# Order of the evictions of v and z at the seam between two head pairs of a differential-attention kernel

## The reference

```
proj = u @ w_in                         # 512x2048 @ 2048x8192
q, k = 16 heads of 128 each;  v = 8 heads of 256;  z = 512x2048
logits = q k^T * 128**-0.5 + rel_bias, causal mask
p = softmax(logits)                     # for both heads of a pair
a = p[head 0] - lam * p[head 1]
o = rms_norm(a @ v, subln_g) * (1 - lam_init)
y = (o * silu(z)) @ w_out
out = layer_norm(alpha * u + y, g, b)
```

## Time and profile before

| | before |
|---|---|
| median of 3 runs | 932.64 us (932.06 to 932.73) |
| the profiled execution's own time | 931.81 us |
| its span | 929.6 us |
| TensorE busy (matmul) | 915.0 us, 98% |
| VectorE busy | 609.9 us, 66% |
| ScalarE busy | 381.3 us, 41% |
| GpSimd busy | 177.8 us, 19% |
| chain that ended last | TensorE 93%, VectorE 5%, ScalarE 1% |

### The profile page before, as it was taken

How to read it: one execution, slowest core, us unless ns; L and a number is a source line. 1 busy time by engine, 2 the same in 40 slices (tenths; PEclk the granted TensorE clock), 3 DMA queues, 4 the chain that set the end, 5 groups by cost and what they waited for, 6 DMA issues and landing times.

```text
span 929.6 us, 14281 instructions
## 1 busy us (share of the span) xinstructions
PE 915.0 (98%) x5210; PEld 807.9 (87%) x5210; DVE 609.9 (66%) x1020; ACT 381.3 (41%) x653; POOL 177.8 (19%) x364
## 2 busy tenths in 40 slices
PE   9999999999999999999999999999999899999996
PEld 8888989898989898989898989898989688888885
DVE  5675767676767576757766675768576877435455
ACT  4443445443535354535453444354534544113211
POOL 1200313031303221222122122312131000000032
PEclk9999999999999999999999999999999999999999
DMA  8732506250625062506250625152517324443332
GB/s 305 285 100 88 188 25 203 86 184 33 198 81 186 23 203 77 183 27 199 82 178 31 195 86 174 37 188 73 159 55 258 139 91 135 182 153 111 133 133 93
DMA packets 43274, 124.53 MB, mean 134 GB/s; under 512 B 8160, under 2 KB 10208, under 8 KB 42992
## 3 DMA queue, kind: packets, MB, share of 16 engines
q1 hardware_dynamic: 29328, 97.27, 31.6%
q0 software_dynamic: 9504, 17.75, 6.0%
q10 hardware_dynamic: 4416, 9.18, 2.7%
HBM read 108.01 MB, written 13.15 MB: 130 GB/s over the span
## 4 chain that ended last, share of the span: by engine, by line
PE 93%; DVE 5%; ACT 1%; DMA 0%; issue 0%; SPq 0%; ACTq 0%; DVEq 0%
PE proj L1401 73%; PE att L1401 20%; DVE scratch L1094 1%; DVE w_split L918 1%; ACT w_split L623 1%; DVE scratch L1087 1%; DVE scratch L1079 1%; DMA w_raw<-w_in_tiles_dram 0%; DVE w_split L924 0%; DVE scratch L1041 0%; DVE operands L1227 0%; DVE operands L1035 0%; DVE big L1393 0%; DVE mix L1073 0%; ACT w_split L632 0%
## 5 line engine op out<-in xcount | busy, mean ns | idle before, releaser
L1401 PE MATMUL proj<-w_split,xg_split 128*128 128x512 f32 (+1 forms) x1512 | 294.4, 354 | 0.0
L1401 PEld LDWEIGHTS proj<-w_split,xg_split 128*128 128x128 f32 x1512 | 250.7, 189 | 39.5
L1401 PE MATMUL proj<-xg_split,w_split 128*128 128x512 f32 (+1 forms) x1032 | 204.2, 355 | 2.7 <-DVE scratch L1041 2.1
L1401 PEld LDWEIGHTS proj<-xg_split,w_split 128*128 128x128 f32 x1032 | 171.4, 189 | 32.1 <-issue 4.6
L918 DVE TENSOR_TENSOR w_split<-w_raw,w_split 128x1024 fp32r<-128x1024 f32 x98 | 119.9, 1223 | 96.0 <-ACT w_split L623 94.4
L623 ACT ACTIVATE w_split<-w_raw 128x1024 fp32r<-128x1024 f32 x98 | 103.7, 1058 | 135.5 <-PE proj L1401 128.5
L549 POOL DMA_DIRECT2D scratch<-scratch x224 | 110.3, 501 | 107.5 <-DVE scratch L1094 57.3
L1401 PE MATMUL att<-w_split,xg_split 128*128 128x512 f32 x432 | 99.9, 389 | 0.0
L1401 PEld LDWEIGHTS att<-w_split,xg_split 128*128 128x128 f32 x432 | 81.0, 188 | 16.8
L623 ACT ACTIVATE w_split<-x_res 128x1024 fp32r<-128x1024 f32 x42 | 44.6, 1061 | 106.0 <-PE proj L1401 67.3
L1401 PE MATMUL proj<-w_split,x_sums 128*128 128x256 f32 x672 | 82.9, 283 | 0.0
(11 more groups left out here) (153 smaller groups left out, 825.3 us busy)
## 6 DMA issues: line engine op xcount, KB each, us to landing
w_raw<-w_in_tiles_dram SPq DMA_DIRECT2D x112, 512.0 KB, 3.6
w_raw<-w_out_tiles_dram SPq DMA_DIRECT2D x32, 512.0 KB, 3.3
x_res<-w_in_tiles_dram SPq DMA_DIRECT2D x14, 512.0 KB, 4.2
bias_by_distance<-bias_lines POOLq DMA_DIRECT2D x8, 640.0 KB, 5.0
scratch<-scratch POOLq DMA_DIRECT2D x112, 40.0 KB, 2.6
bias<-bias_by_distance POOLq DMA_DIRECT2D x8, 512.0 KB, 4.0
x_res<-in_x_dram ACTq DMA_DIRECT2D x4, 1024.0 KB, 6.1
big<-x_cols_dram SPq DMA_DIRECT2D x7, 512.0 KB, 9.6
```

Source lines behind the costliest of these rows:

```text
L1401: return nc.tensor.matmul(dst, lhsT, rhs, start=start, stop=stop, skip_group_check=True)
```

## The change

Four edits, and one instruction.

1. In pairs 0 to 6 VectorE evicts the tile of bank 0 first, then does `combine(p, 3)` and `turn_a(p)`, then the tiles of banks 2, 1 and 3 (`VZ_ORDER`). TensorE's waits count in that order. ScalarE's order stays 0, 1, 2, 3.
2. In pair 7 VectorE evicts tiles 0 and 1 before slot 21, and tiles 2 and 3 behind its block's low part; then come the second early piece of g, the low parts of a for two row tiles, `combine(7, 3)` and the transposition of the last row tile.
3. In pair 7 ScalarE evicts the four banks directly behind slot 21, ahead of the high parts of a and of g's second early piece.
4. The first early piece of g goes to slot 20 on both engines: on ScalarE ahead of the exponentials of the last row tile, on VectorE ahead of the first 16 transpositions.
5. GpSimd gets one `drain()` behind its loop over the pairs.

`weigh_v` and `gate` now wait for all four tiles of v and z, since the counter no longer names a tile.

```
+            nc.gpsimd.drain()                       # GpSimd, behind the loop over the pairs
             for s in range(ST):
...
+                if j == 20 and last_pair(p):        # ScalarE, slot
+                    g_early_hi(0)
                 if 17 <= j < 21:
                     exps(p, j - 17)
...
             for j in range(SLOTS):                  # ScalarE, pair 7
                 slot(PAIRS - 1, j)
+            vz_tiles(PAIRS - 1)
             aT_split(PAIRS - 1, 0)
             aT_split(PAIRS - 1, 1)
-            g_early_hi()
-            vz_tiles(PAIRS - 1)
+            g_early_hi(1)
...
             def vz_tiles(p):                        # VectorE
-                for s in range(ST):
-                    ...
+                vz_tile(p, VZ_ORDER[0])
+                combine(p, 3)
+                turn_a(p)
+                for s in VZ_ORDER[1:]:
+                    vz_tile(p, s)
...
-                if j == 21:                         # VectorE, slot
-                    combine(p, 3)
-                    if not last_pair(p):
-                        turn_a(p)
                 if j == 20 and last_pair(p):
+                    g_early_lo(0)
                     turn_last_a(False)
...
-            for j in range(SLOTS):                  # VectorE, pair 7
+            for j in range(SLOTS - 1):
                 slot(PAIRS - 1, j)
+            vz_tile(PAIRS - 1, 0)
+            vz_tile(PAIRS - 1, 1)
+            slot(PAIRS - 1, SLOTS - 1)
+            vz_tile(PAIRS - 1, 2)
+            vz_tile(PAIRS - 1, 3)
+            g_early_lo(1)
             aT_split(PAIRS - 1, 0)
             aT_split(PAIRS - 1, 1)
-            g_early_lo()
-            vz_tiles(PAIRS - 1)
+            combine(PAIRS - 1, 3)
             turn_last_a(True)
...
-                        pe.wait_ge(vz_moved, p * ST - ST + bank + 1)      # TensorE, opening
+                        pe.wait_ge(vz_moved, p * ST - ST + VZ_ORDER.index(bank) + 1)
...
-                pe.wait_ge(vz_moved, p * ST + tiles[-1] + 1)              # TensorE, weigh_v
+                pe.wait_ge(vz_moved, p * ST + ST)
...
+VZ_ORDER = [0, 2, 1, 3]
```

More of the change, by code:

```diff
@@ L797, in slot, with g_early_hi @@
                     q_chunk(p)
+                if j == 20 and last_pair(p):
+                    g_early_hi(0)
                 if 17 <= j < 21:
                     exps(p, j - 17)
-            def g_early_hi():
+            def g_early_hi(i):
                 act.wait_ge(scores_done, PAIRS * ST)
                 act.wait_ge(g_loaded, 16 * (PAIRS - 1))
-                for i in range(EARLY // 2):
-                    nc.scalar.activation(g_early[:, 0, 2 * i:2 * i + 2], g[:, 2 * i:2 * i + 2],
-                                         ACT.Copy).then_inc(g_hi, 1)
+                nc.scalar.activation(g_early[:, 0, 2 * i:2 * i + 2], g[:, 2 * i:2 * i + 2],
+                                     ACT.Copy).then_inc(g_hi, 1)
             def first_split(i):
@@ L1030, in k_chunk, with vz_tile @@
                                             ALU.subtract).then_inc(k_moved, 1)
+            def vz_tile(p, s):
+                dve.wait_ge(vz_hi, p * ST + s + 1)
+                nc.vector.tensor_tensor(v[:, 1, s], vz_banks(p)[:, s, 0:PW], v[:, 0, s].bitcast(F32), ALU.subtract)
+                twice_silu(p, s).then_inc(first_v_moved if first_pair(p) else vz_moved, 1)
             def vz_tiles(p):
-                for s in range(ST):
[L1034 to L1037, removed]
+                vz_tile(p, VZ_ORDER[0])
[3 more added lines that the diff above has]
+                    vz_tile(p, s)
             def twice_silu(p, t):
@@ L1130, in gate @@
                 dve.wait_ge(first_v_moved, ST)
-                dve.wait_ge(vz_moved, n)
+                dve.wait_ge(vz_moved, p * ST + ST)
                 nc.vector.scalar_tensor_tensor(gated_of(p, t), gated_of(p, t), o_scale[:, t:t + 1], silu_z[:, t],
@@ L1182, in first_slot @@
                     w_sum(1, 0, 3)
-                if j == 15:
-                    combine(0, 3)
-                    turn_a(0)
             def slot(p, j):
@@ L1216, in slot, with g_early_lo @@
                     q_chunk(p)
-                if j == 21:
-                    combine(p, 3)
-                    if not last_pair(p):
-                        turn_a(p)
                 if j == 20 and last_pair(p):
+                    g_early_lo(0)
                     turn_last_a(False)
[L1224 to L1229, removed]
+            def g_early_lo(i):
+                dve.wait_ge(g_hi, i + 1)
+                nc.vector.tensor_tensor(g_early[:, 1, 2 * i:2 * i + 2], g[:, 2 * i:2 * i + 2],
+                                        g_early[:, 0, 2 * i:2 * i + 2].bitcast(F32),
+                                        ALU.subtract).then_inc(g_split, 1)
             def first_split(i):
```

## The result

| | before | changed |
|---|---|---|
| median | 932.43 us (932.06 to 932.73, 4 runs) | 920.61 us (920.48 to 920.67, 4 runs) |
| ratio | | 0.9872 (95%: 0.986 to 0.9884) |
| profiled execution, span | 931.81, 929.6 us | 920.48, 918.4 us |
| TensorE busy | 98% | 99% |
| mean granted clock | 0.998 | 1.000 |

The kernel is 1.3% faster, 11.8 us. The direction and the two large terms came out; a third one, the drain, was put at nothing and is worth 2.3 us. The span became 11.2 us shorter, over the 9.5 that the prediction gave as a sign of being wrong.

What follows compares the result with a forecast made beforehand. TensorE, busy 98% of the span, was taken as the bound, losing time at openings that wait for evictions. Gains of 3.72 + 5.42 = 9.14 us off 932.64 gave 923.5 us, range 921.8 to 927.2.

Steps and rivals of the forecast that it cites:

- the two large terms: Gains at TensorE's openings: 3.72 us in the loop (pairs 2 to 7), 5.42 us at the output projection.
- the drain: GpSimd behind the loop: could gain 0 to 3 us, taken as 0; over 0.5 us had a chance of 0.04.
- sign of being wrong: Wrong if the span's gain exceeds 9.5 us or TensorE's idle time returns under another name for more than 2.
- Edit 1: Openings of pairs 2 to 7: TensorE's wait for bank 0 goes, 6 x 0.62 = 3.72 us gained.
- Edits 2 to 4: Output projection's opening: the 3.55 us wait and the half clock behind it go, 5.42 us gained.
- The tie at step (0, 2): Output stage: VectorE's part of g seen at 748.29, TensorE wants it at 748.32; taken as nothing.
- Slot 20's wait for the reads of g: ScalarE in pair 7 waits for all seven reads of g; margin 0.7 us, cost nothing.
- The subtraction from the median: The 9.14 us gain taken off the median, 932.64 us, which is 0.83 above the profiled execution: 923.5.
- Rival A: TensorE's loop jump was hidden by the wait, so the six openings gain nothing: 927.2 us; chance 0.13.
- B: The last opening's wait moves to step (0, 2): 924.5 to 927.4 us; chance 0.12.
- C: Slower: reads of g land late for ScalarE in slot 20, 933 to 935 us at 10.5 late; chance 0.02.
- D: Loop openings wait for bank 2's tile instead, at worst six times 0.2 us left: 924.7 us; chance 0.05.

Runs made afterwards that it cites:

- e5: Edit 1 alone on the kernel before, without the drain: 928.63 us against 932.41, ratio 0.9959.
- e6: Edits 2 to 4 alone on the kernel before, the loop's evictions as before, no drain: 926.47 us against 932.41.
- e8: The changed kernel with VectorE's first late part of g ahead of its second 16 transpositions: 920.33 us against 920.50.
- e1: The kernel before with the drain alone: 930.38 us against 931.89 on the same chip, ratio 0.998.
- e2: The changed kernel without its drain: 922.86 us.
- e4: The changed kernel with its drain behind pair 3 of GpSimd's loop instead of behind pair 7: 926.23 us.
- e3: The changed kernel with its drain moved to GpSimd's beginning, ahead of every DMA that GpSimd issues: 923.04 us.

## Why the prediction was wrong, point by point

- **Edit 1**, 3.72 us: right. e5 is 3.8 us faster by its medians; in the chain each opening is continuous, and bank 2's tile ended 0.5 us before it was wanted, 0.4 with the semaphore's 0.12 taken off as the forecast did (0.35).
- **Edits 2 to 4**, 5.42 us: right in mechanism and, in the profiled execution, in size. The idle 3.55 is gone and so is the half clock (e6). What I took for a fixed 1.87 us varies from execution to execution; 7.31 and 8.46 us were seen for the same 24 matmuls. "Otherwise it is 1.00" stands in no row shown, but the trace bears it out: the clock is 1.00 but for 741.1 to 744.5 us and the last 0.8 us of the span, behind the work.
- **The tie at step (0, 2)**: "which I take as nothing" was 0.22 us, shown by e8. The second transpositions started 5.6 us behind the output stage's first matmul (738.25 against 732.66; forecast 741.87 against 736.41).
- **Slot 20's wait for the reads of g**: nothing, as said; ScalarE's L807 starts at 723.01, straight behind its block.
- **The drain** is the step that failed. The prediction put it: "Could it gain? [...] 0 to 3 us. I take 0, since GpSimd's rows show it waiting for others only." It is worth 2.3 us (e1, e2), a case that had a chance of 0.04, and with 0 in its place the range's lower end was 921.8. Without its drain the changed kernel takes 922.86 us (e2), inside the range. The reason given was no reason: GpSimd's rows say what it did up to its last instruction, and the question was what followed it. The rows to read were there: GpSimd's last end at 923.90, the last DMA activity at 926.2, the span's end at 929.6. In the last three microseconds no engine and no queue showed anything, and GpSimd was the engine that the change gave a drain. With the 3.4 us from 926.2 to 929.6 as the upper end and their middle as the value, the forecast would have been 921.8 and the range's lower end 920.1, which holds the time; that is said with the result known.
- **The subtraction from the median** was off by 0.7 us. The gain was worked out on the profiled execution, 931.81, and taken off the median, 932.64, so the forecast carried the 0.83 between them over to the changed kernel. There median and profiled execution are 0.13 apart (920.61 and 920.48). This and the drain account for the miss: 923.5 - 2.27 (the drain) - 0.70 (0.83 less 0.13) + 0.22 (the tie) - 0.1 (the start) = 920.65, measured 920.61. Why the kernel before lies above its profiled execution is not shown; a longer stretch at half clock at the last opening, as in e5's trace, would do it, and e6, which takes that opening's stop out, gained 0.7 more than forecast.
- **Rival A** (the loop's jump hidden by the wait): ruled out, 0.00 us of idle time at six openings. The Trainium skill's rule on a taken branch (Runtime: NRT & Kernel Launch, Instruction fetch mechanics), by which the prediction held this rival and 927.2 us, is not borne out on TensorE: the trace does not show its stall.
- **Rivals B, C, D**: B is real with 0.22 us of its 1 to 3.9; C and D did not occur.

## What to carry to other kernels

An engine that waits by order and not by load is found by laying the new order on the old times with the pitch of each instruction; that gave 8.92 us where 8.83 came (8.93 less the 0.1 of the start). The price of a stop of TensorE of 3.5 us was here the stop and 1.9 to 3.0 us more for work at half clock. The runs also lie closer together without it: the sets of runs of a kernel with the stop are 0.7 to 4.1 us apart (before, e1, e5), those without it 0.2 to 0.8, but for 2.0 in e4; that the half clock makes the difference is likely and not shown. And a kernel that issues DMAs from GpSimd should be looked at behind its last instruction: if the span ends microseconds after the last write, put one drain where GpSimd is idle behind its last DMA, not earlier (e3: no gain; e4: 3.4 us slower than none). How much it gives depends on what else ends late: here 2.3 us of a drain's 5.5.

## What the runs showed of the hardware that I had not expected

GpSimd's drain took 3.25, 5.70 and 8.39 us with 38, 68 and 101 of its DMAs since the last one, though all had landed, and 0.12 us directly behind another drain. With 135, 140 and 241 DMAs it took 5.44, 2.85 and 5.46. GpSimd also stopped by itself while issuing, for 2.33 us with 129 DMAs issued and for 1.07 us with 235, or for 1.14 us with 128 issued since a drain, and the drains behind such a stop are the ones that cost less per DMA. Without a drain of the kernel's own, a time of the same size passes at the end of the program: 5.70 us behind GpSimd's last instruction before the change, 8.5 in e4. What exactly is settled at a stop or a drain, and what sets the number, stays open; DMAs of one kind alone, in rising number, would show it and were not tried.
